# Embedding and GLU stage of a hybrid trunk kernel: y fetched in eight rows, input transposed two row tiles to a bank

## The reference

```
e = _rmsnorm(pe @ w_pe, g_pe)              # pe: T x 256, w_pe: 256 x 2048
...
y = jax.nn.gelu(y.reshape(b, t, D_SSM))    # y: T x 1024, already in memory as yT
y = y * jax.nn.sigmoid(y @ w_glu)          # w_glu: 1024 x 1024
ssm * jax.nn.silu(gs)
```

## Time and profile before

| | us |
|---|---|
| median of 3 runs (2385.41 to 2386.32) | 2385.94 |
| the profiled execution | 2386.21 |
| its span | 2384.5 |
| TensorE busy in the span | 2204.8 |
| VectorE busy | 1615.1 |
| ACT busy | 905.3 |

### The profile page before, as it was taken

One profiled execution on the slowest core, in us unless ns is written; L12 is line 12 of the kernel. 1 busy time (PEld: TensorE's weight loads), 2 busy tenths in 40 slices (PEclk: granted clock), 3 DMA queues, 4 the chain that ended last, 5 costly groups with the idle time before them and its releaser, 6 DMA issues. The chain is left out here.

```text
span 2384.5 us, 44150 instructions
## 1 busy us (share of the span) xinstructions
PE 2204.8 (92%) x16355; PEld 2112.5 (89%) x16355; DVE 1615.1 (68%) x2941; ACT 905.3 (38%) x1843; POOL 324.4 (14%) x428
## 2 busy tenths in 40 slices
PE   3999999999899999999889978978989999999995
PEld 3999999999899999999878867978989987889995
DVE  6778766767786888876446646667657666667663
ACT  6542333333533333334366736234343331113112
POOL 0011000000111212111153410001111211111110
PEclk7999999999999999999989989989999999999997
DMA  8484444444757788786377655454556665346332
GB/s 245 145 260 111 141 131 131 149 122 143 263 187 201 225 227 230 221 231 176 112 237 226 204 176 185 131 200 148 190 207 234 217 217 164 110 123 207 103 97 98
DMA packets 362384, 424.80 MB, mean 178 GB/s; under 512 B 76064, under 2 KB 294792, under 8 KB 354336
## 3 DMA queue, kind: packets, MB, share of 16 engines
q1 hardware_dynamic: 306128, 266.62, 37.8%
q0 software_dynamic: 29504, 110.42, 13.5%
q10 hardware_dynamic: 26576, 45.40, 5.9%
HBM read 270.01 MB, written 143.68 MB: 173 GB/s over the span
## 5 line engine op out<-in xcount | busy, mean ns | idle before, releaser
L761 PE MATMUL acc<-t_act,w_hi 128*128 128x264 f32 x5376 | 888.6, 287 | 12.9 <-DVE zb L1323 5.2
L761 PEld LDWEIGHTS acc<-t_act,w_hi 128*128 128x128 f32 x5376 | 749.3, 189 | 19.5 <-issue 18.1
L761 PE MATMUL acc<-t_act,w_lo 128*128 128x264 f32 x2688 | 549.0, 286 | 0.0
L761 PEld LDWEIGHTS acc<-t_act,w_lo 128*128 128x128 f32 x2688 | 418.2, 189 | 0.0
L2764 PE MATMUL m_acc<-m_t_act,m_hi 128*128 128x264 f32 x1792 | 295.7, 288 | 19.4 <-ACT m_acc L2807 9.8
L1316 DVE TENSOR_TENSOR w_lo<-w_raw_f,w_hi 128x512 fp32r<-128x512 f32 x288 | 197.8, 687 | 143.7 <-ACT w_hi L971 143.4
L971 ACT CAST w_hi<-w_raw_f 128x512 fp32r<-128x512 f32 x288 | 177.9, 618 | 265.5 <-PE acc L761 245.0
L2764 PEld LDWEIGHTS m_acc<-m_t_act,m_hi 128*128 128x128 f32 x1792 | 252.7, 191 | 20.0 <-issue 20.0
L3171 PE MATMUL post_acc<-h_hi,w_post_hi 128*128 128x272 f32 (+1 forms) x768 | 210.9, 329 | 7.5 <-PEq L2573 4.3
L3171 PE MATMUL post_acc<-h_hi,w_post_lo 128*128 128x272 f32 (+1 forms) x768 | 208.2, 325 | 0.0
L3171 PE MATMUL post_acc<-h_lo,w_post_hi 128*128 128x272 f32 (+1 forms) x768 | 207.9, 325 | 0.0
(11 more groups left out here) (435 smaller groups left out, 3631.1 us busy)
## 6 DMA issues: line engine op xcount, KB each, us to landing
w_raw_f<-in_w_in_dram SPq DMA_DIRECT2D x96, 512.0 KB, 4.0
w_raw<-in_w_pg_dram SPq DMA_DIRECT2D x64, 512.0 KB, 4.7
cT<-zb SPq DMA_DIRECT2D x24, 1056.0 KB, 4.6
zb<-cT POOLq DMA_DIRECT2D x96, 264.0 KB, 5.8
zT<-zb POOLq DMA_DIRECT2D x80, 264.0 KB, 3.6
m_raw<-in_w_out_dram SPq DMA_DIRECT2D x32, 512.0 KB, 5.8
eT<-e_out ACTq DMA_DIRECT2D x16, 528.0 KB, 3.0
cT<-m_zb SPq DMA_DIRECT2D x8, 1056.0 KB, 5.0
```

The source lines that it names most:

```text
L761: mm = pe.matmul(out[:, c, 0:QN], w[:, k, :], t_act[:, SIDE[r], x, k, c * QN:(c + 1) * QN], start=(opens and k == 0 and m == 0), stop=(k = ...
```

## The change

y is fetched in eight transfers, one per block of 128 rows of yT (528 KB). POOL issues row k when embedding tile k is finished on TensorE and row k-1 has landed; the gs loads stand behind all eight. ACT waits for row k ahead of high_y(k), VectorE ahead of low_y(k), and their single waits ahead of the loops are gone. The transposes go two row tiles to a bank: four to a full bank and two small ones for the sample, five rounds in place of nine, with one ACT copy and one VectorE subtraction each. On VectorE the split of embedding tile 0 stands ahead of the subtractions instead of behind them.

```diff
--- before.py
+++ after.py
@@ -2356,6 +2356,15 @@
         block = ctx.enter_context(nc.Block(no_gpsimd_drain=True))
         w_pe = d["w_pe"][0].rearrange("(k p) n -> p k n", p=P)
         w_glu = d["w_glu"][0].rearrange("(k p) n -> p k n", p=P)
+        PAIRS = [((n, n + 1), P) for n in range(0, TT, 2)] + [((TT,), T_SAMPLE)]
+
+        def turned_part(x, g):
+            tok, width = g * 2 * P, (2 * P if g < TT // 2 else T_SAMPLE)
+            return x[:, :, tok:tok + width]
+
+        def turned_ps(g):
+            return p_ps[g % 2].rearrange("p (k t) -> p k t", k=KP)[:, :, 0:2 * P if g < TT // 2 else T_SAMPLE]
+
         yT = d["yT"].rearrange("r k j -> r (k j)")
 
         @block.sync
@@ -2380,7 +2389,12 @@
             nc.gpsimd.memset(e_sum[:], 0.0).then_inc(ones_set, 1)
             pool.wait_ge(ones_set, 2)
             pool.wait_ge(p_loaded, 32)
-            pool.dma_start(y_raw[:], yT.rearrange("(k p) t -> p k t", p=P)).then_inc(y_loaded, 16)
+            y_rows = yT.rearrange("(k p) t -> p k t", p=P)
+            for k in range(KS):
+                pool.wait_ge(WE.gemm_done, k + 1)
+                if k:
+                    pool.wait_ge(y_loaded, 16 * k)
+                pool.dma_start(y_raw[:, k:k + 1], y_rows[:, k:k + 1]).then_inc(y_loaded, 16)
             with pool.Fori(0, KS // 2) as i:
                 for b in range(2):
                     pool.wait_ge(gated_done[b], i)
@@ -2389,17 +2403,17 @@
 
         @block.tensor
         def _(pe):
-            for n in range(TT + 1):
-                b, rows = n % 2, (P if n < TT else T_SAMPLE)
-                if n == 0:
-                    pe.wait_ge(p_loaded, 32)
-                if n >= 2:
-                    pe.wait_ge(p_lo_done, n - 1)
+            pe.wait_ge(p_loaded, 32)
+            for g, (tiles, rows) in enumerate(PAIRS):
+                if g >= 2:
+                    pe.wait_ge(p_lo_done, g - 1)
                 for k in range(KP):
-                    tr = pe.transpose(p_ps[b][:, k * P:k * P + rows], p_in[0:rows, n, k * P:(k + 1) * P],
-                                      ident[0:rows, 0:rows])
+                    for i, n in enumerate(tiles):
+                        at = (2 * k + i) * P
+                        tr = pe.transpose(p_ps[g % 2][:, at:at + rows], p_in[0:rows, n, k * P:(k + 1) * P],
+                                          ident[0:rows, 0:rows])
                 tr.then_inc(p_turned, 1)
-            pe.wait_ge(p_lo_done, TT + 1)
+            pe.wait_ge(p_lo_done, len(PAIRS))
             with pe.Fori(0, KD // 2) as i:
                 for b in range(2):
                     pe.wait_ge(WE.split[1], i * 2 + (b + 1))
@@ -2427,12 +2441,9 @@
 
         @block.scalar
         def _(act):
-            for n in range(TT + 1):
-                b, rows = n % 2, (P if n < TT else T_SAMPLE)
-                act.wait_ge(p_turned, n + 1)
-                nc.scalar.copy(p_hi[:, :, n * P:n * P + rows],
-                               p_ps[b][:, 0:2 * P].rearrange("p (k t) -> p k t", k=KP)[:, :, 0:rows]) \
-                    .then_inc(p_hi_done, 1)
+            for g, (tiles, rows) in enumerate(PAIRS):
+                act.wait_ge(p_turned, g + 1)
+                nc.scalar.copy(turned_part(p_hi, g), turned_ps(g)).then_inc(p_hi_done, 1)
 
             def embed(m, b, it):
 
@@ -2447,11 +2458,11 @@
 
             def high_y(k):
                 one = bass.ds(k, 1)
+                act.wait_ge(y_loaded, k * 16 + 16)
                 nc.scalar.copy(y_hi[:, one], y_raw[:, one]).then_inc(y_hi_done, 1)
 
             for b in range(2):
                 embed(b, b, 0)
-            act.wait_ge(y_loaded, 16)
             with act.Fori(1, KD // 2) as i:
                 embed(i * 2, 0, i)
                 high_y(i - 1)
@@ -2488,18 +2499,16 @@
         @block.vector
         def _(dve):
             chain = Chain(dve, dve_order)
-            for n in range(TT + 1):
-                b, rows = n % 2, (P if n < TT else T_SAMPLE)
-                dve.wait_ge(p_hi_done, n + 1)
-                nc.vector.tensor_tensor(p_lo[:, :, n * P:n * P + rows],
-                                        p_ps[b][:, 0:2 * P].rearrange("p (k t) -> p k t", k=KP)[:, :, 0:rows],
-                                        p_hi[:, :, n * P:n * P + rows].bitcast(F32), ALU.subtract) \
-                    .then_inc(p_lo_done, 1)
             WE.split_tile(dve, nc, 0, 0, False)
+            for g in range(len(PAIRS)):
+                dve.wait_ge(p_hi_done, g + 1)
+                nc.vector.tensor_tensor(turned_part(p_lo, g), turned_ps(g), turned_part(p_hi, g).bitcast(F32),
+                                        ALU.subtract).then_inc(p_lo_done, 1)
             WE.split_tile(dve, nc, 1, 1, False)
 
             def low_y(k):
                 one = bass.ds(k, 1)
+                dve.wait_ge(y_loaded, k * 16 + 16)
                 dve.wait_ge(y_hi_done, k + 1)
                 nc.vector.tensor_tensor(y_lo[:, one], y_raw[:, one], y_hi[:, one].bitcast(F32), ALU.subtract) \
                     .then_inc(y_split, 1)
@@ -2514,7 +2523,6 @@
             WE.split_tile(dve, nc, 2, 0, True)
             WE.split_tile(dve, nc, 3, 1, True)
             add_squares(0, 0)
-            dve.wait_ge(y_loaded, 16)
             with dve.Fori(1, KD // 2 - 1) as i:
                 WE.split_tile(dve, nc, i * 2 + 2, 0, True)
                 add_squares(1, i - 1)
```

## The result

The changed kernel is slower: 2391.95 us median of 17 runs (2388.16 to 2395.42), the kernel before 2385.66 in 17 runs beside it (2379.90 to 2392.30). The ratio is 1.0024, with a 95% interval of 1.0016 to 1.0033. The forecast was 2382.4, and the range ended at 2389.

The account below looks back on a forecast made before the run. The side stage was taken as bound by TensorE, its early hole waiting for weights beside y, then by the single-buffer load/split ring. 7.55 us saved less 4.0 for rows gave 3.55 net: 2382.4 us, range 2377.5 to 2389.

Parts of the forecast that it names:

- Start: Transposes up to embedding tile 0: banked transposes and the split placed ahead start tile 0 at about 1421.95, 0.4 us saved.
- The hole: TensorE's wait ahead of embedding tile 1: without y in flight, tile 0 to tile 2 takes 8.05 us, 6.75 saved.
- The gain without the rows: Side stage, start plus hole plus 0.4 us at tiles 2 and 3: together 7.55 us saved.
- the price of the rows: Embedding loop: rows 2 to 7 delay weight loads by 0.5 us a tile over 8.3 tiles, 4.0 us in all.
- rows 0 and 1: Early embedding tiles: TensorE is the bound and weights wait for it, so these two rows cost nothing.
- the chance: Weight loads in the loop: a row is in motion 46% of the time, a load meeting it pays half of 2.2 us.
- the gs pair: gs loads on POOL move from 1416.6 to about 1464, cost nothing in lateness; their load delays are within the 4.0 us.
- Every load pays: Split and load ring, tiles 6 to 14: 2.2 us a tile, 2396.6 us; decides above 0.9 a tile; chance 0.11.
- Rows come late: ACT's high_y waits for rows, TensorE behind it: decides above 7.7 us a row, 2389 at 9 us; chance 0.05.
- Rows cost nothing: Embedding loop: rows fall into idle DMA time and the 7.55 us stays, 2378.4 us; chance 0.40.
- batching rule: Splitting y into rows: the rule gives 3.2 us a row, 26 in series against 12 whole; the sum does not change.

Follow-up runs that it names:

- e5: Changed kernel with y in three pieces on SP's queue behind the weights of tiles 0, 1, 2, gs held until all embedding tiles finish: stage 66.33 us, ratio 0.9974.
- e8: Changed kernel with gs held until embedding ends and row k issued once ACT has evacuated tile 2k: stage 74.70 us, ratio 1.0002.
- e2: Changed kernel with the gs loads held on POOL until all 16 embedding tiles are finished: stage 77.09 us, ratio 1.0022.
- e3: Changed kernel with gs held until embedding ends, each row transfer an eighth of its columns, rest of y zeroed by memset: stage 73.04 us, ratio 0.9997.

## Why the prediction was wrong

*The gain was right.* Start: 0.4 forecast, 0.54 measured. The hole: 14.80 became 8.51, where I had 8.05; the clock rose in tile 1, not ahead of it (the x3 at 1424.42 takes 0.83 us). The gain without the rows was put at 7.55 us; e5 shows 7.7 (74.05 - 66.33). That the sum fits so closely is luck, for its terms do not: in e5 tile 0 to tile 2 takes 7.33 us (8.05 forecast), and tiles 2 and 3 take 6.28, as before (5.9 forecast).

*The step that failed is the price of the rows*, "half of 2.2 as the mean for a load that falls into it: 0.5 us a tile ... 8.3 tiles: 4.0 us, the two gs loads behind row 7 included". It measured 13.9, with e5 as the base. (8.3 times 0.5 would be 4.15; that slip changes nothing.) Three things in it were wrong.

First, "rows 0 and 1 fall where TensorE is the bound and weights wait for it, so they are free". Tiles 2 and 3 took 8.93 us in place of the 5.9 forecast: VectorE's splits of tiles 3 and 4 waited for halves that landed 3.5 and 4.5 us after issue. The single raw buffer lets a load begin only when the split before is done. Tile 3's load left when tile 1 had begun, and that one load beside row 0 used up the lead of the weights: tile 3 waited 0.39 us, tile 4 2.28.

Second, the chance. I took a row to be in motion in 46% of the time and a load to fall into it at random. They are not independent. In the changed kernel the loads of tiles 4 to 9 each leave within half a us of a row and come in about when it lands, as the casts and issues above show, and rows that stand apart still cost 1.05 us each on average (e8), against 1.35 in a train. The bound of 2.2 us from the earlier trace rows held: the loads of tiles 3, 4 and 6, beside rows, took 3.5 to 4.5 us, against a median of 2.4 before. The factor on it did not.

Third, the gs pair. I moved it from 1416.6 to about 1464, asked only when it is wanted, and counted it with the rows. It follows row 7 with no wait for a landing, and with three transfers in one go the load of tile 10 took 5.9 us and the clock was lost behind the hole. Holding the pair back gave 3.2 us (e2).

*The rivals.* "Every load pays" is what happened, with tiles at 4.6 to 5.1 us from 4 to 9 against 3.74; its deciding point, 0.9 us a tile, was passed. I gave it 0.11 because a row seemed rare in time, which was the wrong measure. "Rows come late" did not happen: rows landed in 4.6 us (5.0 forecast), and ACT's four waits for them are 0.7 each, as long as its waits of the earlier trace rows for its own passes. "Rows cost nothing" fell with the first row.

The sentence on the batching rule of the Trainium skill (DMA: Bandwidth & Descriptors, Bandwidth) said its price was low here. The trace agrees as far as the rows' arrival goes: a row took 4.6 us, more than the 3.2 estimated from the Trainium skill, and no wait of ACT for one was longer than 0.7. What decided is not in that rule: the price was paid by the weight loads beside the rows.

## What to carry to other kernels

Where a ring of load, split, load with one buffer is on the path, a bulk transfer beside it is paid by the load that it meets. Here that was 1.05 to 1.35 us for every 528 KB, while with eight transfers of 66 KB in the loop the stage was 1.0 us longer than with none (59.81 in e3, 58.81 in e5). Price it per transfer and by its size, not by the share of time that the engines are busy. Put bulk data where the next load is wanted late, here into the start of the stage at half clock, rather than spreading it over the loop that is bound by loads. When a transfer is moved, ask what it runs into at its new place, and not only when it is wanted there.

## What was not expected of the hardware

In e3 a memset on POOL held VectorE. The timelines of DVE and POOL:

```profile
1413.29 6.41 DVE L140 CAST w_pe_s_hi<-w_pe_s_raw 128x128 fp32r<-128x128 f32 x2 [6.22 <-DMA w_pe_s_raw<-in_w_pe_dram]
...
1412.42 7.14 POOL L2390 MEMSET y_raw<- 128x8448 f32 x1
```

Two casts that take 0.36 us elsewhere end at 1419.70, 0.14 us after the memset (1412.42 + 7.14 = 1419.56). The Trainium skill (SBUF — State Buffer, SBUF: two separate sides) says that GpSimd and VectorE share a port pair, and that whichever starts first holds it alone for its whole instruction, if VectorE's is one in a two-port mode. The trace agrees with a lock held to the memset's end; whether the cast runs in such a mode no row here shows. Tile 0 came 5.7 us later for it.
